# A hybrid block with latent attention: heads in pairs, scores two heads ahead, and q and k heads laid out over all 128 rows

## The chip, the cores and the metric

The kernel runs on one core of one Trainium2 chip. The metric is the device time of one execution in microseconds. The median of 3 runs of the kernel before is 1793.98 us (1790.98 to 1795.46). TensorE (PE) multiplies matrices into the eight banks of PSUM, VectorE (DVE), ScalarE (ACT) and GpSimd (POOL) work on tiles of 128 rows, and SyncE (SP) issues most of the loads.

## The reference, cut to what matters

Two layers follow each other: a first block (gated linear attention, a state space layer, a feed-forward network) and a second block. The change is in the second block's attention, with 512 tokens, 8 heads, 64 plain and 32 rotated dimensions for each head of q and k, and 64 for v. Beside it runs a depthwise convolution with a layer norm. In words, from the reference:

```python
q, kv = rmsnorm(q_lat, q_norm_g) @ w_uq, rmsnorm(kv_lat, kv_norm_g) @ w_ukv   # 384 -> 8*96, 256 -> 8*128
q_pe, k_pe = apply_rope(q[..., 64:96], cos, sin), apply_rope(k_rope, cos, sin)  # k_pe is one for all heads
s = jnp.einsum('bhqd,bhkd->bhqk', q_blk, k) * 96 ** -0.5
p = jax.nn.softmax(jnp.where(mask, s, neg), axis=-1)                            # mask: position of the key <= that of the query
o = jnp.einsum('bhqk,bhkd->bhqd', p, v)                                         # then @ w_o_attn
def apply_rope(x, cos, sin):
    x1, x2 = jnp.split(x, 2, axis=-1)
    return jnp.concatenate([x1 * cos - x2 * sin, x2 * cos + x1 * sin], axis=-1)
```

The attention output and the normed, gated (silu) convolution each go through a projection of 512 to 1024 (`oa` and `oc` below), are gated, added and go through `w_out` (`wo2`). A mixture of experts ends the block.

## The kernel before, in words

All weights come in units of 128x2048 through a ring of three tiles, in the order of `PLAN` (around the change: ga, gc, uq 0, uq 1, kv 0, oa 0, oa 1, oc 0, oc 1, wo2). Each unit is split into a high and a low part: ScalarE copies the high part (`high`, L953), then VectorE or POOL subtracts it (`low`, L1557). POOL does it for ga, gc, uq and kv, VectorE for oa, oc and wo2. A product then is three matmuls, high x high, high x low, low x high (`three`). The high and low parts have two places, used in turn, so the high part of a unit can be written once the unit two before it is used. `next_high(name, i)` and `next_low(name, i)` stand where the split of the unit after `name, i` is issued.

Every engine has its own program in a fixed order, written out by hand: `tensor`, `scalar`, `vector`, `gpsimd`, `sync`. Nothing is moved past a wait. Each instruction signals by name (`sig`) and others wait for the name (`at`). `Banks` gives out the PSUM banks, the one closed longest ago first; the taker waits until the last reader of the old tile has freed it. One bank, `conv`, is VectorE's accumulator for the convolution until `banks.close("conv")`.

The stretch around the change, in order:

- *q.* TensorE makes 8 tiles of 128x512, one for each head: rows 0 to 63 the plain dimensions, 64 to 95 the rotated, 96 to 127 the rotated with halves exchanged. ScalarE copies the first 64 rows to `QH` (L1383). VectorE multiplies rows 64 to 95 by the cosine and 96 to 127 by the signed sine and adds them (`rope`, L2167, L2168, L2170). POOL copies the rotated k to all heads (L2605) between its two weight splits.
- *k.* TensorE makes 8 tiles of 64x512, ScalarE copies them to `KH` (L1387).
- *Scores.* `scores(h)` makes 4 tiles of 128 queries x 512 keys in fp32; a fp32 matmul shows in the trace as two passes. `v2` follows scores(0).
- *Softmax.* On VectorE `soften(h)` scales and masks (L2225), takes the row maximum (L2228) and negates it (L2230), for each tile; ScalarE takes the exponential with the sum (L1393); VectorE normalises (L2235, L2238).
- *Output.* TensorE transposes the probabilities (L769, 16 for a head), ScalarE copies them to `PT` (L1405), TensorE multiplies by v into half of a bank (`pv`); two heads fill it, and ScalarE and VectorE take its high and low part (L1410, L2263).
- In the loop over heads TensorE does scores(h + 1), then the transposes of h, then the product with v of h.
- *Convolution.* Its mean, centring (L2257), squares (L1414), variance, square root (L979), reciprocal (L1569), norm (L2245, L2247), sigmoid (L1422) and POOL's product (L2610) are spread over the heads. `cvh` and `cvl` are its high and low part.
- After the loop come oa (2 units), oc (2 units) and wo2 (4 units). The first unit of oa is consumed for each of the four pieces of the attention output as it comes.

Of the kernel before, what the change touches and what calls it, by code (L numbers as in the profile page):

```python
# [7 lines left out]
F32 = mybir.dt.float32  # L8
# [4 lines left out]
ALU = mybir.AluOpType  # L13
# [134 lines left out]
def program(nc, W, wmoe, mcst, vecs, cst, xT, wal, wgu, bc, rw, posr, posc, xslot, yslot, prep, bbar, ushuf, yshuf, out):  # L148
    ctx = ExitStack()
    with ctx:  # L150
# [64 lines left out]
        def con(name):  # L215
# [68 lines left out]
        PB = [[tile(f"probs{z}{m}", o, 512) for m, o in enumerate(oo)]  # L284
              for z, oo in enumerate(((14336, 14848, 15360, 15872), (16384, 21112, 22648, 23160)))]
        PT = [tile(f"probs_t{k}", 29816 + 512 * k, 512) for k in range(4)]
# [69 lines left out]
        ogf = RO["og"].rearrange("p m g -> p (m g)")  # L356

# [3 lines left out]
        def tensor(g):  # L361
# [367 lines left out]
            for h in range(8):  # L729
                b = fresh("kh", h)  # L730
                for k in range(2):
                    t = three(b[0:64, :], wh[:, k, 64 * h:64 * h + 64], wl[:, k, 64 * h:64 * h + 64], kvh[:, k, :], kvl[:, k, :], k == 0, k == 1)
                t.then_inc(*p.sig(("kh", h)))
                banks.close("kh", h)
            p.end("end", "heads", "pe")

            def scores(h):
                p.wait_ge(*at("kh_ready"))
                p.wait_ge(*at("rope_ready"))
# [14 lines left out]
            banks.close("conv")  # L754
            b = fresh("conv_mean")
# [5 lines left out]
            for h in range(8):  # L761
                z = h % 2
                if h < 7:
                    scores(h + 1)
                for kb in range(4):
                    b = fresh("pt", h, kb)
                    for m in range(4):
                        p.wait_ge(*at("probs", h, m))
                        t = g.transpose(b[:, 128 * m:128 * m + 128], PB[z][m][:, 128 * kb:128 * kb + 128], ident)  # L769
                    t.then_inc(*p.sig(("pt", h, kb), ("turned", h)))  # L770
                    banks.close("pt", h, kb)
                b = fresh("pv", h // 2) if h % 2 == 0 else banks.at("pv", h // 2)
                o = b[64 * (h % 2):64 * (h % 2) + 64, :]
                p.wait_ge(*at("v2_ready"))
                p.wait_ge(*at("probs_t", h))
                for kb in range(4):
                    t = mm(o, V2[:, kb, 64 * h:64 * h + 64], PT[kb], kb == 0, kb == 3)
                t.then_inc(*p.sig(("pv", h // 2), ("attended", h)))
                if h % 2:
                    banks.close("pv", h // 2)  # L780
                if h == 1:
# [164 lines left out]
        def scalar(g):  # L946
# [432 lines left out]
            for i in range(2):  # L1379
                next_high("uq", i)  # L1380
                for h in range(4 * i, 4 * i + 4):
                    a.wait_ge(*at("uq", h, 0))
                    g.activation(QH[0:64, h, :], banks.at("uq", h, 0)[0:64, :], ACT.Copy).then_inc(*a.sig(("uq_out", h)))  # L1383
# [1487 lines left out]
```

## Time and profile before

| what | value |
|---|---|
| median of 3 runs | 1793.98 us |
| span of the profiled execution (its own time is not given apart from it) | 1789.8 us |
| TensorE busy | 1691.9 us, 95% |
| VectorE busy | 1219.3 us, 68% |
| ScalarE busy | 744.2 us, 42% |
| POOL busy | 352.4 us, 20% |
| mean granted TensorE clock | 0.973 |

The profile is one execution. The span goes from its first to its last instruction. A busy share is an average over stages with different limits, so the stages are read one by one, in windows of us from the start of the span.

### The profile page before, as it was taken

The page shows a single profiled execution, that of the slowest core. Times are in us where ns is not written, and L with a number is a line of the kernel's source. Part 1 is how long each engine was busy: PE and PEld are TensorE (multiplying, and loading weights), DVE is VectorE, ACT ScalarE, POOL GpSimd, SP SyncE. Part 2 cuts the span into 40 slices and gives each one's busy share as a digit, 9 for nine tenths or more (in the row PEclk, how much of TensorE's full clock was granted, in tenths as well). Part 3 has the DMA queues.
Part 4 walks back from the last instruction along what each step waited for, and adds up shares of the span by engine and source line. Part 5 has one row for each costly group of instructions (what it writes and reads, how often), then busy time and mean ns, then how long its engine had stood idle before and what let it go on. Part 6 is the DMA issues. An engine that isn't in the chain of part 4 may idle for free. (4 is left out here: it accounts for less than half of the span.)

```text
span 1789.8 us, 19686 instructions
## 1 busy us (share of the span) xinstructions
PE 1691.9 (95%) x8122; PEld 1330.9 (74%) x8122; DVE 1219.3 (68%) x1585; ACT 744.2 (42%) x962; POOL 352.4 (20%) x193
## 2 busy tenths in 40 slices
PE   6999899899999989999999989999898998999997
PEld 5778777677888868888878877878543776777775
DVE  5979768963333349843555446959786565999998
ACT  5253445444222342222222224342466235777774
POOL 1000012114000004200000014433200002555552
PEclk8999999999999999999999969999998999999999
DMA  6425222423322324434435402222100104999995
GB/s 231 182 100 181 75 73 72 160 82 129 118 94 94 128 84 164 165 133 184 153 143 186 165 24 78 94 93 94 71 0 1 71 24 157 397 380 385 384 367 192
DMA packets 59641, 264.51 MB, mean 148 GB/s; under 512 B 21648, under 2 KB 22288, under 8 KB 33056
## 3 DMA queue, kind: packets, MB, share of 16 engines
q1 hardware_dynamic: 34896, 159.10, 24.3%
q0 software_dynamic: 15184, 99.90, 14.2%
q10 hardware_dynamic: 9472, 4.26, 0.8%
q8 instruction: 64, 1.05, 0.2%
q14 instruction: 25, 0.20, 0.0%
HBM read 239.80 MB, written 23.44 MB: 147 GB/s over the span
## 5 line engine op out<-in xcount | busy, mean ns | idle before, releaser
L372 PE MATMUL bank<-h_high,wsplit 128*128 128x512 f32 x992 | 321.6, 402 | 10.9 <-ACT h_high L1283 4.9
L1557 DVE TENSOR_TENSOR wsplit<-ring,wsplit 128x2048 fp32r<-128x2048 f32 x75 | 174.3, 2324 | 160.4 <-ACT wsplit L953 160.4
L953 ACT ACTIVATE wsplit<-ring 128x2048 fp32r<-128x2048 f32 x98 | 187.0, 1908 | 210.8 <-PE bank L372 198.1
L372 PEld LDWEIGHTS bank<-h_high,wsplit 128*128 128x128 f32 x992 | 189.1, 191 | 57.4 <-ACT h_high L1283 5.0
L372 PE MATMUL bank<-xn_high,wsplit 128*128 128x512 f32 (+1 forms) x832 | 218.0, 349 | 11.3 <-DVE xn_low L1588 8.0
L372 PE MATMUL bank<-h_low,wsplit 128*128 128x512 f32 x496 | 198.1, 399 | 0.0
L372 PEld LDWEIGHTS bank<-xn_high,wsplit 128*128 128x128 f32 x832 | 146.2, 191 | 33.8 <-DVE xn_low L1588 8.1
L372 PE MATMUL bank<-f_high,wsplit 128*128 128x512 f32 x512 | 168.2, 401 | 0.0
L372 PE MATMUL bank<-xn_low,wsplit 128*128 128x512 f32 (+1 forms) x416 | 144.2, 347 | 0.0
L1557 POOL TENSOR_TENSOR wsplit<-ring,wsplit 128x2048 fp32r<-128x2048 f32 x23 | 106.3, 4622 | 179.1 <-ACT wsplit L953 178.9
L2620 POOL DMA_INDIRECT ring<-in_wmoe,indices x42 | 84.4, 2010 | 187.3 <-DVE routing L2362 135.3
L2579 POOL TENSOR_TENSOR x<-x,z 128x512 f32<-128x512 f32 x8 | 11.5, 1441 | 552.8 <-DVE z L2032 552.8
L372 PEld LDWEIGHTS bank<-f_high,wsplit 128*128 128x128 f32 x512 | 96.3, 188 | 21.9
L372 PEld LDWEIGHTS bank<-h_low,wsplit 128*128 128x128 f32 x496 | 94.9, 191 | 22.3 <-issue 0.2
L372 PE MATMUL bank<-f_low,wsplit 128*128 128x512 f32 x256 | 101.2, 395 | 0.0
L2157 DVE SCALAR_TENSOR_TENSOR bank<-conv_in,vecs,bank 128x512 f32<-128x512 f32 x116 | 87.7, 756 | 4.1
L372 PEld LDWEIGHTS bank<-xn_low,wsplit 128*128 128x128 f32 x416 | 79.4, 191 | 10.7 <-issue 1.0
L372 PE MATMUL bank<-m_high,wsplit 128*128 128x512 f32 x256 | 81.4, 396 | 3.8 <-DVE wsplit L1557 2.9
L372 PE MATMUL bank<-g_high,wsplit 128*128 128x512 f32 x256 | 80.8, 395 | 0.0
L372 PE MATMUL bank<-wsplit,block_high 128*128 128x512 f32 x232 | 76.2, 410 | 0.6 <-DVE block_low L2419 0.6
L1293 ACT ACTIVATE f_high<-norm_tmp 128x512 fp32r<-128x512 f32 x32 | 20.3, 634 | 123.5 <-DVE norm_tmp L2091 123.5
L372 PE MATMUL bank<-parts,block_high 128*128 128x512 f32 x216 | 68.9, 400 | 0.0
(496 smaller groups left out, 3398.9 us busy)
## 6 DMA issues: line engine op xcount, KB each, us to landing
ring<-in_W SPq DMA_DIRECT2D x122, 1024.0 KB, 4.8
weights_out<-prep SPq DMA_DIRECT2D x8, 864.0 KB, 5.4
prep<-weights_out_early POOLq DMA_DIRECT2D x8, 576.0 KB, 3.1
xslot<-zeros SPq DMA_DIRECT2D x7, 516.0 KB, 5.1
block<-xslot SPq DMA_DIRECT2D x6, 516.0 KB
yslot<-block_out SPq DMA_DIRECT2D x6, 512.0 KB, 9.1
prep<-turns_early POOLq DMA_DIRECT2D x8, 288.0 KB, 2.4
x_in<-in_xT SPq DMA_DIRECT2D x4, 528.0 KB, 7.4
```

Of the source, the lines that this page charges most:

```text
L372: return g.matmul(o, l, r, start=first, stop=last_, skip_group_check=True)
L953: g.activation(wst[:, side(n), 0, :], ringt[:, n % RING, :], ACT.Copy).then_inc(*a.sig(("high", n)))
L1293: g.activation(fh[:, j % 16, :], nrm[:, 2 * z, :], ACT.Square).then_inc(*a.sig(("f_high", j)))
L1557: g.tensor_tensor(wst[:, side(n), 1, :], ringt[:, n % RING, :], hi, SUB).then_inc(*t.sig(("low", n), ("released", n)))
L2157: g.scalar_tensor_tensor(out=o, in0=i, scalar=cw[:, c, k:k + 1], in1=grown, op0=MUL, op1=ADD).then_inc(*v.sig(("convolved",), ("free", "co ...
L2579: g.tensor_tensor(X[:, k, :], X[:, k, :], Z[:, k, :], ADD).then_inc(*q.sig((name, "x", k)))
L2620: g.indirect_dma_start(slots[c % NS], None, wmoe, indexed(x)).then_inc(slot_landed[c % NS], 16)
```

## The change

It does the following.

- q: the columns of `w_uq` are laid out by fours of heads: one tile with the rotated dimensions of four heads (4 x 32 rows), one with the exchanged ones, two with the plain ones of two heads each. VectorE multiplies the first two over 128 rows, and adds by head. ScalarE copies the plain ones, freeing the banks.
- k: 4 products with 128 columns in place of 8 with 64.
- Softmax: one `tensor_tensor_reduce` for each tile makes the negated, scaled and masked scores and their minimum; the exponential takes them with a scale of -1.
- The loop goes by pairs of heads. Scores run two heads ahead, probabilities have 10 tiles in place of 8, turned ones 8 in place of 4, and both heads' products with v alternate between the halves of a bank.
- The convolution's root is taken after head 5 (the variance is copied plainly before), its norm after the last normalise, and its sigmoids after the loop. The split of oa 1 moves into the loop.

```diff
-        PB = [[tile(f"probs{z}{m}", o, 512) for m, o in enumerate(oo)]
-              for z, oo in enumerate(((14336, ...), (16384, ...)))]
-        PT = [tile(f"probs_t{k}", 29816 + 512 * k, 512) for k in range(4)]
+        PB = [tile(f"probs{k}", o, 512) for k, o in enumerate((14336, 14848, ... 28280))]       # 10
+        PT = [tile(f"probs_t{k}", o, 512) for k, o in enumerate((29816, 30328, ... 29304))]     # 8
+        def probs(h, m):
+            return PB[(4 * h + m) % 10]
 tensor:
-            for h in range(8):
-                b = fresh("kh", h)
+            for j in range(4):
+                b = fresh("kh", j)
                 for k in range(2):
-                    t = three(b[0:64, :], wh[:, k, 64 * h:64 * h + 64], ...)
+                    t = three(b, wh[:, k, 128 * j:128 * j + 128], ...)
 ...
             banks.close("conv")
+            scores(1)
             b = fresh("conv_mean")
 ...
+            def attend(pr):
+                b = fresh("pv", pr)
+                p.wait_ge(*at("v2_ready"))
+                p.wait_ge(*at("probs_t", 2 * pr + 1))
+                for kb in range(4):
+                    for e in range(2):
+                        h = 2 * pr + e
+                        t = mm(b[64 * e:64 * e + 64, :], V2[:, kb, 64 * h:64 * h + 64], PT[4 * e + kb], kb == 0, kb == 3)
+                        if kb == 3:
+                            t.then_inc(*p.sig(("pv", pr), ("attended", pr)))
+                banks.close("pv", pr)
+            for pr in range(4):
+                for h in (2 * pr, 2 * pr + 1):
+                    turn_probs(h)                      # the 16 transposes
+                    if h < 6:
+                        scores(h + 2)
+                attend(pr)
+                if pr == 1:                            # conv_var
 scalar:
+                    j, e = 4 * i + 2 + (h % 4) // 2, h % 2
+                    g.activation(QH[0:64, h, :], banks.at("uq", j, 0)[64 * e:64 * e + 64, :], ACT.Copy)
 ...
             soften(0)                                  # V2 copies follow
+            soften(1)
             for h in range(8):
+                probs_out(h)                           # the 4 copies to PT
+                if h < 6:
+                    soften(h + 2)
                 if h % 2:
+                    a.wait_ge(*at("attended", h // 2)) # copy to ath
+                if h == 1:                             # 4 squares of the convolution, then
+                    next_high("oa", 0)
+                elif h == 3:
+                    g.activation(rs, banks.at("conv_var"), ACT.Copy)
+                elif h == 5:
+                    g.activation(rs, rs, ACT.Sqrt, scale=1.0 / 512, bias=eps)
+            for c in range(4):                         # the 4 sigmoids
+                g.activation(nrm[:, c % 3, :], CO[:, c, :], ACT.Sigmoid)
             a.wait_ge(*at("end", "attention", "pe"))   # 4 copies to cvh
-            for i in range(2):
-                next_high("oa", i)
+            next_high("oa", 1)
 vector:
-                for h in range(4 * i, 4 * i + 4):
-                    rope(QH[64:96, h, :], banks.at("uq", h, 0), ("free", "uq", h, 0))
+                for z in range(2):
+                    g.tensor_tensor(KP[:, z, :], banks.at("uq", 4 * i + z, 0), TR[:, z, :], MUL)
+                for e in range(4):
+                    r = slice(32 * e, 32 * e + 32)
+                    g.tensor_tensor(QH[64:96, 4 * i + e, :], KP[r, 0, :], KP[r, 1, :], ADD)
 ...
-                    g.scalar_tensor_tensor(out=pb, in0=banks.at("s", h, m), scalar=96.0 ** -0.5, in1=MK[:, m, :], op0=MUL, op1=ADD)
-                    g.tensor_reduce(mx, pb, AX, MAX)
-                    g.tensor_scalar(mx, mx, -1.0, None, MUL)
+                    if n > 9:                          # n = 4 * h + m
+                        v.wait_ge(*at("turned", (n - 10) // 4))
+                    g.tensor_tensor_reduce(out=probs(h, m), in0=banks.at("s", h, m), in1=MK[:, m, :], scale=-(96.0 ** -0.5), scalar=-BIG,
+                                           op0=ADD, op1=ALU.min, accum_out=st[:, z, m:m + 1])
 ...
             soften(0)
+            soften(1)
+            for pr in range(4):
+                normalise(2 * pr)
+                normalise(2 * pr + 1)
+                if pr == 0:                            # wait for conv_mean, centre 4 tiles
+                else:                                  # low part of pair pr - 1
+                if pr == 1:
+                    next_low("oa", 0)
+                if pr < 3:
+                    soften(2 * pr + 2)
+                    soften(2 * pr + 3)
+            for c in range(4):
+                conv_norm(c)
+            v.wait_ge(*at("at_high", 3))               # low part of pair 3
+            oa_out(0)                                  # then the 4 low parts of the convolution,
+            next_low("oa", 1)                          # then
+            oa_out(1)
```

## Rows read from the trace of the kernel before

**Rows 1.** The page: busy time of the engines.

```profile
PE 1691.9 (95%) x8122; PEld 1330.9 (74%) x8122; DVE 1219.3 (68%) x1585; ACT 744.2 (42%) x962; POOL 352.4 (20%) x193
```

**Rows 2.** Windows of stages: busy us (instructions) by engine, granted clock, DMA.

```profile
1250.00:1268.00 18.00, 15.97 (x68) 12.17 (x66) 14.84 (x12) 7.87 (x10) 13.33 (x3) 1.00 0.16 59
1268.00:1283.00 15.00, 12.24 (x49) 6.18 (x49) 13.20 (x17) 6.91 (x11) 0.02 (x1) 1.00 0.19 71
...
1298.00:1386.00 88.00, 76.62 (x252) 35.45 (x251) 65.98 (x132) 57.38 (x111) 5.43 (x4) 0.94 0.00 0
...
1386.00:1409.00 23.00, 23.00 (x99) 18.54 (x100) 12.89 (x15) 6.47 (x8) 0.00 (x0) 1.00 0.26 92
```

**Rows 3.** Timeline of PE, k products and first scores: start us, us.

```profile
1268.36 0.39 PE L372 MATMUL bank<-kv_low,wsplit 128*64 128x512 f32 x1
...
1274.70 0.44 PE L372 MATMUL bank<-kv_high,wsplit 128*64 128x512 f32 x1 [0.67 <-DVE rope_tmp L2168]
...
1282.90 3.70 PE L372 MATMUL bank<-kh,qh 96*128 96x512 f32 x8 [0.68 <-ACT kh L1387]
```

**Rows 4.** Timeline of POOL in the head of the stretch.

```profile
1254.44 4.57 POOL L1557 TENSOR_TENSOR wsplit<-ring,wsplit 128x2048 fp32r<-128x2048 f32 x1 [9.53 <-ACT wsplit L953]
1259.16 3.86 POOL L2605 COPY kh<-k_pe 32x4096 f32<-32x4096 f32 x1 [0.15 <-POOL wsplit L1557]
1263.10 4.92 POOL L1557 TENSOR_TENSOR wsplit<-ring,wsplit 128x2048 fp32r<-128x2048 f32 x1
```

**Rows 5.** Timeline of DVE there: end of the convolution, rope, the split.

```profile
1251.57 0.75 DVE L2157 SCALAR_TENSOR_TENSOR conv<-conv_in,vecs,bank 128x512 f32<-128x512 f32 x1
...
1256.40 3.16 DVE L2170 TENSOR_TENSOR qh<-rope_tmp 32x512 f32<-32x512 f32 x1
...
1279.93 2.29 DVE L1557 TENSOR_TENSOR wsplit<-ring,wsplit 128x2048 fp32r<-128x2048 f32 x1
```

**Rows 6.** Timeline of PE in the loop: one head, and the last two.

```profile
1305.22 3.70 PE L372 MATMUL bank<-kh,qh 96*128 96x512 f32 x8
1308.75 1.91 PE L769 MATMUL bank<-cst,probs 128*128 128x128 f32 x16
1311.51 3.65 PE L372 MATMUL bank<-probs_t,v 128*64 128x512 f32 x8 [0.85 <-ACT probs_t L1405]
1315.09 3.70 PE L372 MATMUL bank<-norm_tmp,cst 128*128 128x512 f32 x8
...
1375.88 3.64 PE L769 MATMUL bank<-cst,probs 128*128 128x128 f32 x16 [1.36 <-DVE probs L2238]
1380.21 5.70 PE L372 MATMUL bank<-probs_t,v 128*64 128x512 f32 x8 [0.69 <-ACT probs_t L1405]
```

**Rows 7.** Windows at the end of the loop, as rows 2.

```profile
1378.00:1380.00 2.00, 1.52 (x8) 1.12 (x6) 0.00 (x0) 1.49 (x3) 0.00 (x0) 0.50 0.00 0
```

**Rows 8.** Groups by line from 1282 to 1386: busy, mean ns, idle before.

```profile
L2228 DVE TENSOR_REDUCE small<-probs 128x1 f32<-128x512 f32 x32 | 22.0, 686 | 1.1
L2225 DVE SCALAR_TENSOR_TENSOR probs<-bank,mask 128x512 f32<-128x512 f32 x32 | 21.8, 682 | 3.3 <-PE bank L372 3.3
...
L2238 DVE TENSOR_SCALAR probs<-probs,small 128x512 f32<-128x512 f32 x32 | 16.4, 576 | 0.3
...
L1393 ACT ACT_TABLE_LOAD x6 | 7.7, 1283 | 0.1
L1393 ACT ACTIVATION_READ_ACCUMULATOR probs<-probs,small 128x1 f32 x32 | 6.1, 192 | 0.0
...
L1422 ACT ACT_TABLE_LOAD x4 | 5.1, 1283 | 0.1
...
L1569 DVE RECIPROCAL norm_tmp<-norm_tmp 128x512 f32<-128x512 f32 x1 | 3.3, 3343 | 0.0
```

**Rows 9.** Timeline of ACT in the head of the stretch: copies of q.

```profile
1254.18 1.65 ACT L1383 ACTIVATE qh<-bank 64x512 f32<-64x512 f32 x3
```

**Rows 10.** The state products of the first block (`into`): timeline of PE.

```profile
277.49 1.15 PE L372 MATMUL bank<-u_shuffled,g_turned 128*64 128x65 f32 x32
```

More of the change, by code:

```diff
@@ L738, in scores @@
                 p.wait_ge(*at("kh_ready"))
+                p.wait_ge(*at("nope_ready"))
                 p.wait_ge(*at("rope_ready"))
@@ L760, in tensor, with turn_probs @@
             banks.close("conv_mean")
[L761 to L764, printed above, removed]
+            def turn_probs(h):
                 for kb in range(4):
@@ L2210, in vector @@
                 next_low("uq", i)
-                for h in range(4 * i, 4 * i + 4):
-                    v.wait_ge(*at("uq", h, 0))
-                    v.wait_ge(*at("uq_out", h))
-                    rope(QH[64:96, h, :], banks.at("uq", h, 0), ("free", "uq", h, 0))
+                for z in range(2):
+                    v.wait_ge(*at("uq", 4 * i + z, 0))
+                    v.wait_ge(*v.own())
+                    g.tensor_tensor(KP[:, z, :], banks.at("uq", 4 * i + z, 0), TR[:, z, :], MUL).then_inc(*v.sig(("free", "uq", 4 * i + z, 0)))
+                v.wait_ge(*v.own())
+                for e in range(4):
+                    r = slice(32 * e, 32 * e + 32)
+                    g.tensor_tensor(QH[64:96, 4 * i + e, :], KP[r, 0, :], KP[r, 1, :], ADD).then_inc(*v.sig(("rope_ready",)))
             next_low("kv", 0)
@@ L2251, in vector @@
             soften(0)
-            for h in range(8):
-                normalise(h)
-                if h == 0:
+            soften(1)
[3 more added lines that the diff above has]
+                if pr == 0:
                     v.wait_ge(*at("conv_mean"))
@@ L2276, in vector @@
                     g.tensor_tensor(GA[:, j, :], banks.at("oa", j, 0), GA[:, j, :], MUL).then_inc(*v.sig(("free", "oa", j, 0)))
+            oa_out(0)
+            for c in range(4):
+                v.wait_ge(*at("cv_high", c))
+                g.tensor_tensor(cvl[:, c, :], CO[:, c, :], cvh[:, c, :].bitcast(F32), SUB).then_inc(*v.sig(("cv_split", c)))
+            next_low("oa", 1)
+            oa_out(1)
             for i in range(2):
@@ L2826, in layout @@
     q = a["w_uq_2"][0].reshape(384, 8, 96)
-    q = lay(np.concatenate([q, q[:, :, 80:96], q[:, :, 64:80]], axis=2).reshape(384, 1024), 512)
+    turned_q = np.concatenate([q[:, :, 80:96], q[:, :, 64:80]], axis=2)
+    q = lay(np.concatenate([x[:, 4 * i:4 * i + 4].reshape(384, -1) for i in range(2) for x in (q[:, :, 64:96], turned_q, q[:, :, 0:64])], axis=1), 512)
     parts["uq"] = np.concatenate([q, np.zeros((2, 128, 512), np.float32)], axis=2)
```

98 lines of the change are left out of this document (39 added, 59 removed).

## The prediction, before the changed kernel was run

> **What bounds the kernel now.** I read the page first: TensorE is busy for 95% of the span, so time is won only where it waits or does less [rows 1]. Then the windows, one for each stage around the change. The reader is to see that TensorE is full until 1250, has gaps from 1250 to 1283 (15.97 of 18 us, 12.24 of 15 us) and in the attention loop (76.62 of 88 us, at a granted clock of 0.94), and is full again from 1386 to 1409 [rows 2]. So about 137 us, from the first q product at 1248.5 to the first product of the attention output at 1385.8, are where this change can act; what runs after it is a chain of its own.
>
> Then the timelines of the engines in that stretch. **Head of the stretch:** the k products start at 1268.08, when POOL has split their weights, and three of them wait 0.67 us for VectorE's rope to free a bank [rows 3, 4]. The scores start at 1282.90 behind the last k copy [rows 3]. VectorE does three rope instructions for each head, on 32 rows. Three of the sums take 2.4 to 3.4 us where 512 elements take 0.68 (L2225) [rows 8], and each ends 0.54 us after a POOL instruction ends (1259.56 after 1259.01, 1263.57 after 1263.02, 1268.56 after 1268.02) [rows 4, 5]: a sum of two SBUF tiles stands still while POOL works. **Loop:** a head costs TensorE 3.5 us of scores, 1.8 us of transposes, 0.9 us of waiting for the copies of the turned probabilities and 3.55 us of products with v (1305.22, 1308.75, 1311.51, 1315.09) [rows 6]: 9.9 us. 8 of these, with 5.5 us for v2 and twice 3.5 us for the convolution's mean and variance, would be 91.5 us; the stretch from 1282.9 to 1385.8 is 102.9. The other 11 us are waits for normalised probabilities, and a half clock at the end: the same 16 transposes take 3.64 us and the same products 5.70 us, with the granted clock at 0.50 (the 1.2 GHz level) after a wait of 1.4 us and several of about 1 us [rows 6, 7]. The waits come from VectorE: 0.68 + 0.69 + 0.15 us, 1.51 us from start to start, for each of 32 score tiles, and from ScalarE's ten table loads of 1.28 us [rows 8].
>
> **The change part by part.** I make a schedule from durations of rows.
>
> *Rope and k.* VectorE: 24 instructions become 4 products of 0.69 us and 8 sums of 0.68 us. It is done with the convolution at 1252.3, and its first two products end at 1253.8 [rows 5]. Of the first four sums, at worst one gets through between two POOL instructions, so they end at 1259.6, 1263.6 and 1268.6; the next two products and four sums take 6 x 0.72 us, to 1272.9, and the split of oa's first unit, 2.29 us, ends at 1275.2. TensorE: the k products start at 1268.07 as before, since POOL's chain of 4.57, 3.86 and 4.92 us sets that and is not touched. There are 24 instead of 48, at 0.233 us (1268.36 to 1269.05 is three of them): they end at 1273.7, and the banks that they take are free by 1269.3. ScalarE: the last q tile is there just before the k products start, two copies follow, the split of the next unit runs from 1268.8 to 1270.7, then 8 copies at 0.55 us (three took 1.65) [rows 9], to 1275.1. So the scores start at 1275.1, set by ScalarE's copies; VectorE is free when the first score tile is ready, over 1 us after (two passes). Gain 7.8 us.
>
> *Softmax.* Three instructions for a tile become one that reads the same PSUM tile and mask and also writes the row minimum. The trace shows no such instruction. Below: it can't be quicker than the 0.68 us of L2225, which is the same read and write. Above: a second pass, 0.68 + 0.69. Nearest is L2225, with a small read of the sum as ScalarE has (0.19 us, L1393) [rows 8]. I take 0.8 us. The Trainium skill ("VectorE: DVE Perf Modes", Two Vector instructions with no wait between them) says that an instruction that also gives out its accumulator is two, the second a read without input. No row of VectorE shows it; by it the whole would be 1 to 2 us longer, within the range.
>
> *Products with v.* They go in pairs of heads, alternately into rows 0 to 63 and 64 to 127 of a bank: 16 passes for a pair. The trace before has one place with such alternation, the state products of the first block (`into`): 32 passes of 65 columns in 1.15 us, so (1.15 - 0.22) / 31 = 0.030 us each, 0.46 ns a column. The products with v, not alternating, run at 0.43 us for 512 columns, 0.84 ns a column [rows 6, 10]. So two halves of the array run side by side, at 1.8 times the rate. Two ends: 16 x 512 x 0.46 = 3.8 us for a pair, or 16 x 0.43 = 6.9 us. I take the 3.8, as the alternation there is the same, though its passes are short. The Trainium skill ("TensorE: Matmul & The Clock Gate", Part 3: Packing small matmuls) gives 2.38 times for three column tiles. By that efficiency two tiles would give 1.6 times and 4.4 us for a pair, 2 us more in the whole.
>
> *Order.* Scores run two heads ahead, so the copies of the turned probabilities lie behind scores, except for the last pair. ScalarE's table loads between exponentials go: the root's value is copied plainly and the four sigmoids come after the loop. The final normalisation of the convolution (reciprocal 3.34 us, then four times two instructions, 1.25 us) moves behind the last normalise.
>
> *The sum*, from the start of the scores, T = 0. TensorE: scores 0 to 3.5, v2 to 9.0, scores to 12.4, mean to 15.8. VectorE has softened head 1 by 13.7 and normalised head 0 by 15.5 (four of L2238, 0.58 us in the mean with POOL's products in the way, and a small reciprocal; I take 1.9 us a head, without POOL [rows 8]), so nothing waits. Turn, scores, turn, scores, pair 0: 17.6, 21.1, 22.8, 26.3, 30.1. Head 2's probabilities are ready at 29.8: turn to 31.9, scores to 35.3. Here ScalarE is late: it has copied pair 0's output (31.2), squared four tiles (33.4) and split oa's second unit (35.3) before it copies head 2's turned tiles (37.4), exponentiates head 4 (41.3) and copies head 3's (43.4). Pair 1 can't start before 43.4, where TensorE would have been ready at about 41.5: to 47.2. Variance 50.7; turn, scores, turn, scores, pair 2: 52.4, 55.9, 57.6, 61.1, 64.9. VectorE finishes head 7's scores at 62.5 and its normalise at 66.3: turns to 66.6 and 68.4. ScalarE has the root with its table load until 67.6, then eight copies, as those of q some 0.5 us each: 71.8. Pair 3 ends at 75.7. I add 1.3 us for semaphore steps that I left out: 77. The half clock at the end I expect once more, because TensorE waits 3.5 us there; at half speed over the last pair and its neighbours it costs 2 us, where before it cost (3.64 - 1.91) + (5.70 - 3.62) and 1.4 us more on head 6, 5.2 us inside the 102.9. That gives 79.
>
> *After the loop* nothing is won. The convolution's chain now starts at the end of the loop: table load 1.28, sigmoid 0.63, four POOL products of 1.4 and the copies are done 9 us later, VectorE's lows after oa's first outputs at 17, and the split of oc's first unit at 19.3, while oa's 96 products keep TensorE until 22.5 as now. Cover is 3 us; if it were gone, each us would cost one.
>
> So 7.8 + 102.9 - 79 = 31.7 us; I say 31. The profiled execution had a span of 1789.8 us, 4.2 under the median of 1793.98 us of the runs shown; only its span is given. The stretch is the same in both, so I take the gain from the median: 1763 us.
>
> **The rivals.** *The halves of the array do not overlap* in long fp32 passes that accumulate: 4 x (6.9 - 3.8) = 12.4 us more, all on TensorE's path, as ScalarE's late chain starts from pair 0's end and moves with it. 1775 us. For it: the only row with overlap has passes of 65 columns. Against it: the rate there. Chance 0.18.
> *VectorE's new instruction takes two passes* (1.4 us): a pair costs it 8 x 1.4 + 3.8 + 0.7 = 15.7 us against TensorE's 14.3 us, so VectorE sets the loop; stretch near 83, 1768 us. Chance 0.10.
> *The convolution's chain becomes the end*: 6 us more after the loop, if ScalarE's sigmoids or POOL's products wait longer than summed: 1769 us. Chance 0.06.
> *Slower*: the new instruction runs at the pace of the reciprocal, 3.34 us for 128x512 [rows 8]. With 32 on VectorE's path the loop is 81 us at 1.5 us each and 32 us longer for each us more: the gain is gone from 2.4 us on, and at 3.34 the stretch is 140 us, 1823 us. Nothing else that reads PSUM takes so long here. Chance 0.04.
> The forecast itself: 0.62.
>
> **How the numbers follow.** A measurement of this kernel can't tell less than 0.3%, 5.4 us, from no change; that bound is 1788.6 us. The forecast's own range is 1757 to 1768 (instruction 0.68 to 1.0 us, half clock none or twice). To take in both middle rivals and the first one with 3 us to spare the range is 1755 to 1778. Faster 0.93: the forecast, the three milder rivals but for 0.03 where several of these costs add up to no change; slower 0.04.
>
> **What would show each step right or wrong.** The k products as 24 and scores starting near 1275 (not 1283). Rope sums stretched by POOL only up to 1268.6. A pair's products, 16 passes, in about 4 us, not 7. The new VectorE instruction under 0.9 us. Three table loads in the stretch, not ten or more. TensorE's first oa product near 1354, with its one longer wait ahead of the last pair; oc's first product 22.5 us after it, without a wait. Wrong would be a VectorE busy throughout the loop, or a TensorE wait on the convolution's lows.

## The result, and the profile after

The changed kernel takes 1758.14 us (median of 4 runs) where the kernel before took 1792.74 us beside it (4 runs): a ratio of 0.9822, with a 95% interval of 0.9803 to 0.984. The prediction was 1763 us, in a range of 1755 to 1778. The profiled execution took 1757.74 us, with a span of 1755.7 us.

The page of the changed kernel, busy time of the engines, to be set beside [rows 1]:

```profile
span 1755.7 us, 19580 instructions
...
PE 1664.1 (95%) x8098; PEld 1322.3 (75%) x8098; DVE 1189.1 (68%) x1541; ACT 735.0 (42%) x955; POOL 340.0 (19%) x193
```

TensorE has the same share of a shorter span, so what it does got shorter too, by 27.8 us. The timeline of TensorE after the change, in the stretch from the first q product to the first product of oa (start us, us, instruction, number; in brackets the wait and who ended it), answers to [rows 3, 6]:

```profile
1268.58 0.50 PE L376 MATMUL bank<-kv_high,wsplit 128*128 128x512 f32 x1 [0.36 <-POOL wsplit L1583]
...
1276.27 3.70 PE L376 MATMUL bank<-kh,qh 96*128 96x512 f32 x8 [1.83 <-ACT kh L1404]
...
1302.65 3.65 PE L376 MATMUL bank<-probs_t,v 128*64 128x512 f32 x16
1306.23 1.97 PE L773 MATMUL bank<-cst,probs 128*128 128x128 f32 x16
...
1313.84 3.70 PE L376 MATMUL bank<-kh,qh 96*128 96x512 f32 x8 [0.33 <-DVE small L2255]
1318.82 3.65 PE L376 MATMUL bank<-probs_t,v 128*64 128x512 f32 x16 [1.28 <-ACT probs_t L1419]
...
1339.98 3.71 PE L773 MATMUL bank<-cst,probs 128*128 128x128 f32 x32
1346.80 5.16 PE L376 MATMUL bank<-probs_t,v 128*64 128x512 f32 x16 [3.10 <-ACT probs_t L1419]
1351.88 22.66 PE L376 MATMUL bank<-attn,wsplit 128*128 128x512 f32 x96
```

Three things are to be seen. Sixteen passes of probabilities by v, for two heads, take 3.58 us from start to start (1302.65 to 1306.23), as long as eight took before. The reader can tick off the long waits: one of 1.83 us ahead of the scores, one of 1.28 us ahead of pair 1, and one of 3.10 us ahead of pair 3, all for ScalarE's copies. Pair 3 then runs at half clock, 5.16 instead of 3.65 us. Its windows show it (us from the start; busy us of each engine with the number of instructions, granted clock, DMA):

```profile
1346.00:1352.00 6.00, 5.20 (x17) 1.69 (x18) 4.82 (x9) 0.66 (x2) 0.00 (x0) 0.72 0.00 0
1352.00:1375.00 23.00, 23.00 (x99) 18.54 (x100) 10.30 (x14) 8.90 (x12) 5.19 (x4) 1.00 0.14 46
```

VectorE's timeline after, for the rope's sums, the split of oa's first unit, and the new instruction (L2255):

```profile
1254.39 14.68 DVE L2244 TENSOR_TENSOR qh<-rope_tmp 32x512 f32<-32x512 f32 x4
...
1270.70 2.83 DVE L2244 TENSOR_TENSOR qh<-rope_tmp 32x512 f32<-32x512 f32 x4
1273.57 2.29 DVE L1583 TENSOR_TENSOR wsplit<-ring,wsplit 128x2048 fp32r<-128x2048 f32 x1
...
1313.70 0.68 DVE L2255 CUSTOM_DVE_ANT_0 probs<-bank,mask 128x512 f32<-128x512 f32 x1
1314.31 0.08 DVE L2255 DVE_READ_ACCUMULATOR2_ANT small<- 128x1 f32 x1
```

The first four sums take 14.68 us beside POOL's three instructions, the next four, with POOL idle, 2.83 us. The fused instruction is 0.68 us of work and 0.08 us to read the minimum. The next tile's work starts 0.61 us after it where nothing holds VectorE.

How the stretches compare is the key to all that follows, so they are set out once. All are differences of start times on TensorE's timeline of one profiled execution each. Times of the whole are less sharp: the first q product comes between 1246.26 and 1253.45 us in the 12 profiles, though no kernel here changes anything ahead of it that was meant to take time.

| kernel | time, us | first q product | to first scores | from there to first oa product | from there to the end of the span |
|---|---|---|---|---|---|
| before | 1792.74 | 1248.73 | 34.17 | 102.93 | 404.0 |
| after | 1758.14 | 1249.15 | 27.12 | 75.61 | 403.8 |
| e1, not alternating | 1767.99 | 1252.06 | 27.11 | 84.00 | 403.5 |
| e2, three instructions | 1771.94 | 1253.45 | 27.12 | 85.38 | 404.7 |
| e3, old heads | 1765.82 | 1253.31 | 34.17 | 75.81 | 403.9 |
| e4, heads only | 1784.71 | 1250.42 | 27.11 | 99.77 | 403.9 |
| e5, fused only | 1787.75 | 1250.10 | 34.19 | 97.83 | 403.0 |
| e6, order alone | 1775.52 | 1248.27 | 28.67 | 95.55 | 402.5 |
| e7, late root | 1755.19 | 1247.67 | 27.12 | 72.16 | 404.4 |
| e8, all moves | 1752.28 | 1249.16 | 27.06 | 70.18 | 403.4 |
| e9, scores per head | 1747.43 | 1246.26 | 26.06 | 69.98 | 402.8 |
| e10, passes per copy | 1749.60 | 1252.89 | 25.13 | 68.77 | 403.6 |

One run of e1 (2073.95 us, mean granted clock 0.744) and one of e5 (2302.36 us, 0.675) were slow: they are in the medians of the table, which would be 1767.26 and 1787.52 us without them, and not in the ratios below.

The result in these terms: 7.05 us come from the head of the stretch and 27.32 us from the loop, 34.4 us, and nothing from what follows. The spans differ by 34.1 us, the medians by 34.6 us.

### The profile page after: what moved, and what is told of

Read it like the earlier page. It is cut to its first block and busy times, and to the rows that moved or that the text cites. A ratio compares the mean times of both kernels' runs of the same rounds, so it can differ in the third digit from the quotient of the medians.

```text
span 1755.7 us, 19580 instructions
## 1 busy us (share of the span) xinstructions
PE 1664.1 (95%) x8098; PEld 1322.3 (75%) x8098; DVE 1189.1 (68%) x1541; ACT 735.0 (42%) x955; POOL 340.0 (19%) x193
## 3 DMA queue, kind: packets, MB, share of 16 engines
q1 hardware_dynamic: 34896, 159.10, 25.1%
## 5 line engine op out<-in xcount | busy, mean ns | idle before, releaser
L376 PE MATMUL bank<-h_high,wsplit 128*128 128x512 f32 x992 | 320.6, 401 | 10.8 <-DVE h_low L2070 4.9
L2617 POOL TENSOR_TENSOR x<-x,z 128x512 f32<-128x512 f32 x8 | 11.6, 1444 | 554.3 <-DVE z L2058 554.3
L376 PEld LDWEIGHTS bank<-xn_low,wsplit 128*128 128x128 f32 x416 | 79.0, 190 | 10.8 <-issue 1.0
```

The lines of the kernel that those rows point to most:

```text
L376: return g.matmul(o, l, r, start=first, stop=last_, skip_group_check=True)
L2617: g.tensor_tensor(X[:, k, :], X[:, k, :], Z[:, k, :], ADD).then_inc(*q.sig((name, "x", k)))
```

## The experiments

The first four kernels ran on one chip beside the kernel before (1790.41 us, 13 runs), e5 to e8 on another (1789.24 us, 15 runs), e9 and e10 in a third set (1788.35 us, 9 runs). Ratios are to the kernel before on the same chip, with the 95% interval.

### e1: a pair's heads one after the other

```diff
-                for kb in range(4):
-                    for e in range(2):
+                for e in range(2):
+                    for kb in range(4):
```

> The changed kernel, with the 4 products of the even head done before the 4 of the odd one, as before the change. If TensorE's own work sets the loop and the alternation runs two halves of the array at once, a pair's 16 passes take 7.1 us from start to start instead of 3.6, four times, so 14 us more: 1772 us, the stretch from the first scores to the first oa product 89.6 us instead of 75.6. If the softmax chain sets the loop, TensorE's waits before pair 1 (1.3 us) and pair 3 (3.1 us) and more would swallow part: 10 us more or less. If the passes were quick for another reason than the alternation, 3.6 us stays.

1767.99 us, ratio 0.9868 (0.9847 to 0.9889). The loop is 8.4 us longer than after, and not the 14 of my first case. A pair takes 5.35 us from start to start (1305.55 to 1310.90). TensorE's weight loads of that pair (start us, us, number in the group) say why:

```profile
1306.89 0.14 PEld L376 LDWEIGHTS bank<-probs_t,v 128*64 128x64 f32 x1 [0.29 <-issue]
1307.32 0.19 PEld L376 LDWEIGHTS bank<-probs_t,v 128*64 128x64 f32 x3 [0.29 <-issue]
1307.75 0.19 PEld L376 LDWEIGHTS bank<-probs_t,v 128*64 128x64 f32 x2 [0.23 <-issue]
1308.18 0.19 PEld L376 LDWEIGHTS bank<-probs_t,v 128*64 128x64 f32 x2 [0.23 <-issue]
1308.66 0.14 PEld L376 LDWEIGHTS bank<-probs_t,v 128*64 128x64 f32 x1 [0.29 <-issue]
```

Every 0.43 us one load, but from 1307.32 on there are two or three, and then one again. The rows do not name the head, but one load in each of these steps makes up the first head's eight, and the other four must be the second head's, for the other half of the array. The passes themselves start likewise: two at 1307.32, then at 1307.75 and 1307.80, 1308.18 and 1308.23, 1308.60 and 1308.66, and from 1309.09 on one each 0.43 us. So four of the sixteen passes run beside others without any alternation: 12 steps of 0.43 us, 5.2 us, where with alternation there are 8 steps. Of the 8.4 us, 1.8 are in each of the first three pairs, and the rest in the last one, which runs at half clock in both kernels (8.35 against 5.16 us). That the halves overlap is shown, and the overlap does not even need the alternation to begin. Why it begins four passes ahead, and not earlier, stays open.

### e2: three softmax instructions in the new order

The exponential's scale of -1 goes back with them.

```diff
-                    g.tensor_tensor_reduce(out=probs(h, m), in0=banks.at("s", h, m), in1=MK[:, m, :], scale=-(96.0 ** -0.5), scalar=-BIG,
-                                           op0=ADD, op1=ALU.min, accum_out=st[:, z, m:m + 1])
+                    g.scalar_tensor_tensor(out=pb, in0=banks.at("s", h, m), scalar=96.0 ** -0.5, in1=MK[:, m, :], op0=MUL, op1=ADD)
+                    g.tensor_reduce(mx, pb, AX, MAX)
+                    g.tensor_scalar(mx, mx, -1.0, None, MUL)
```

> The changed kernel, with scaling and mask, row maximum and negation as three VectorE instructions again. A tile costs VectorE 1.51 us instead of 0.61 to 0.86, a pair 8 x 1.51 + 3.6 + 0.7 = 16.4 us against TensorE's 14.0 us. If TensorE's work set the loop, VectorE now does: 8 to 10 us more, 1767 us. If the gain of the loop came mostly from the quicker softmax, it goes back by more than 15 us. If VectorE had slack all along, under 3 us.

1771.94 us, ratio 0.9909 (0.9878 to 0.9941). The loop is 9.8 us longer than after, in the 8 to 10 expected. The whole is 5 us above the 1767 expected; in the profile 4.3 us of that lie ahead of the first q product. VectorE now sets the loop's pace, as TensorE's timeline shows: scores wait for it tile by tile, and pair 1 waits for what follows from it.

```profile
1324.56 1.12 PE L376 MATMUL bank<-kh,qh 96*128 96x512 f32 x2 [0.18 <-DVE probs L2256]
1326.07 1.12 PE L376 MATMUL bank<-kh,qh 96*128 96x512 f32 x2 [0.38 <-DVE probs L2256]
...
1331.36 5.15 PE L376 MATMUL bank<-probs_t,v 128*64 128x512 f32 x16 [2.67 <-ACT probs_t L1419]
```

From 1324.56 to 1326.07 is 1.51 us, VectorE's pace for a tile with three instructions [rows 8].

### e3 and e4: the heads' layout alone

e3 is the changed kernel with the old layout of q and k, e4 is the kernel before with the new one:

```diff
-            for h in range(8):
-                b = fresh("kh", h)
+            for j in range(4):
+                b = fresh("kh", j)
```

and with it the tables of q's columns, VectorE's rope and ScalarE's copies, as in the change (e4; e3 the other way).

> The changed kernel, with q and k laid out and handled as before (8 q tiles with rope for each head, 8 k tiles of 64 rows). The scores start at 1283 instead of 1276, and the loop is the same: 7 us more, 1765 us. Rival: the head of the stretch is hidden, as the loop has its own end set by the convolution or by ScalarE: under 2 us.

> The kernel before with the new layout of q and k alone. If the two halves of the change add up, 7 us less than before: 1786 us, scores at 1276, and the loop of 102.9 us the same from there. Rival: the start comes earlier, but the loop grows by what VectorE has to catch up (the split of oa's first unit now falls into the start of the softmax): 3 us less.

e3: 1765.82 us, ratio 0.986 (0.9841 to 0.9879). e4: 1784.71 us, ratio 0.997 (0.9955 to 0.9984). By the table the layout is worth 7.05 us of head in either kernel, and in the new order nothing more. In the old order the loop is 3.2 us shorter as well, where I had expected no change, but no part of that can be put down to the layout: it is where the waits and the half clock fell in the two profiles. TensorE's timeline of e4 at the end, to be set beside [rows 6]:

```profile
1365.16 5.57 PE L372 MATMUL bank<-probs_t,v 128*64 128x512 f32 x8 [0.78 <-ACT probs_t L1409]
1370.66 2.21 PE L770 MATMUL bank<-cst,probs 128*128 128x128 f32 x16
1373.72 3.65 PE L372 MATMUL bank<-probs_t,v 128*64 128x512 f32 x8 [0.84 <-ACT probs_t L1409]
```

The slow passes (5.57 us) stand one head earlier than in the kernel before, and cost 3.2 us in all (0.96 in the transposes ahead of them, 1.92 and 0.30) where before they cost 5.1. Behind them the wait of 1.36 us for normalised probabilities is gone, as the probabilities were normalised while the slow passes ran. Together that is the 3.2 us of the loop.

### e5: the fused instruction alone, in the old order

The kernel before with the instruction of e2's diff the other way round, and a scale of -1 in the exponential.

> The kernel before with one edit: VectorE's three softmax instructions become the one, as in the changed kernel. Order of the loop, layout of the heads and all else are old. Theory (TensorE bounds the loop): the waits for normalised probabilities go, and with them the half clock; heads one after the other without overlap of halves leave 8 x (3.7 scores + 6.9 probabilities by v) + 8 x 3.7 turning, some 94 to 96 us from first scores to first product of oa where before had 102.9. So about 8 us less than before: near 1784. Rival (ScalarE's reloading of tables and its chain through each head bound the old loop anyway): at most 3 us, near 1789.

1787.75 us (10 runs), ratio 0.999 (0.9977 to 1.0002): no change that can be told. My theory expected 8 us, the rival at most 3, and the rival has it. TensorE's timeline of two heads late in the loop:

```profile
1365.22 0.72 PE L769 MATMUL bank<-cst,probs 128*128 128x128 f32 x2
1367.02 2.04 PE L769 MATMUL bank<-cst,probs 128*128 128x128 f32 x14 [1.07 <-DVE probs L2235]
1369.99 3.62 PE L372 MATMUL bank<-probs_t,v 128*64 128x512 f32 x8 [0.94 <-ACT probs_t L1405]
1374.96 2.73 PE L769 MATMUL bank<-cst,probs 128*128 128x128 f32 x16 [1.36 <-DVE probs L2235]
1378.54 3.65 PE L372 MATMUL bank<-probs_t,v 128*64 128x512 f32 x8 [0.84 <-ACT probs_t L1405]
```

The waits for normalised probabilities are still there, 1.07 us (and once more at 1345.17) and, as before [rows 6], 1.36 us, with VectorE busy for 31.80 of 60 us (1292 to 1352) where before it had 49.23. Only a wait of 0.47 us, at 1332.85 in the kernel before, is gone. What VectorE, POOL and ScalarE did ahead of these waits (timelines of the same kernel):

```profile
1362.69 0.69 DVE L2260 TENSOR_TENSOR attn<-bank,attn 128x512 fp32r<-128x512 f32 x1 [6.09 <-ACT attn L1410]
1363.29 0.68 DVE L2242 TENSOR_TENSOR conv<-conv,norm_tmp 128x512 f32<-128x512 f32 x1
...
1364.68 2.68 DVE L2235 TENSOR_SCALAR probs<-probs,small 128x512 f32<-128x512 f32 x4
1365.30 1.38 POOL L2607 TENSOR_TENSOR conv<-conv,norm_tmp 128x512 f32<-128x512 f32 x1 [9.77 <-ACT norm_tmp L1422]
1365.48 1.48 DVE L2235 TENSOR_SCALAR probs<-probs,small 128x512 f32<-128x512 f32 x1
...
1369.86 1.28 ACT L1393 ACT_TABLE_LOAD   x1
...
1374.12 0.18 DVE L2232 RECIPROCAL small<-small 128x4 f32<-128x4 f32 x1 [4.32 <-ACT probs L1393]
```

VectorE stood idle for 6.09 us, until ScalarE had copied the pair's output, and only then came its queue: the low part of the pair, two instructions of the convolution, the reciprocal and the normalisation. So these waits do not come from how much VectorE does. They have two origins.

- *1.07 us, twice.* Of the four normalisations the third (the row at 1365.48, one of the four of the row at 1364.68) takes 1.48 us where the others take 0.48, while POOL multiplies for the convolution (1365.30 to 1366.68). TensorE has turned two blocks and waits for the third tile. The same third normalisation is stretched at 1343.63 in this kernel, and twice in the kernel before, each time beside POOL's product. VectorE's queue brings the two together: head 6's exponentials were done at 1362.17, before the low part and the convolution began.
- *1.36 us, once.* VectorE had waited 4.32 us for the exponentials, and ScalarE had loaded a table (1.28 us) between its copies and them.

No run took POOL's product or the table load alone out of the old order, so both origins are read from the timelines and not tested.

The profiled loop is 5.1 us shorter; 4.3 of them are the half clock, which cost the kernel before 5.1 us at its last two heads (3.35 for 2.04, 3.64 for 1.91, 5.70 for 3.65 us) and e5 0.8 (2.73 for 1.91). The medians are 1.7 us apart (1789.24 and 1787.52), so not all of this is there in every execution.

### e6: the order without the two others

The changed kernel with both edits of e1 and e2.

> The changed kernel with the three softmax instructions and with a pair's sixteen passes head by head: of the loop only the order (pairs, scores two heads ahead) is new; the layout of q and k stays new. Runs so far gave +9.8 us for the three instructions alone and +8.4 for the lost alternation alone, over 75.6 from first scores to first product of oa. Theory (the loop goes by whichever engine is slower in each pair): VectorE is slower with three instructions, so TensorE's longer passes hide behind it: 86 to 89 us, near 1773. Rival (both lie on one chain, as a pair's passes hold the scores that VectorE waits for): the costs add, 94 us, near 1780.

1775.52 us, ratio 0.9921 (0.9898 to 0.9943). The loop takes 95.55 us: the costs add (9.8 and 8.4 on top of 75.6 are 93.8), as the rival had it for the loop; the time of the whole lies between the two, nearer to my theory's 1773. My expectation that the longer passes would hide behind VectorE is wrong. One reason can be read, at one place: while TensorE runs pair 1's passes and the variance it makes no scores, and VectorE, the slower one, waits for the next ones.

```profile
1344.35 0.69 DVE L2256 SCALAR_TENSOR_TENSOR probs<-bank,mask 128x512 f32<-128x512 f32 x1 [4.92 <-PE bank L376]
```

Behind pair 0 VectorE waited for ScalarE's split instead (2.65 us, to 1319.75). Another reason is again the clock. Pair 1 takes 7.06 us (the granted clock is 0.50 from 1332 to 1334), and so does the last pair. The first scores take 5.40 us for 3.70. The head of the stretch, 28.67 us, has a half clock too, in q products from 1259.95 to 1263.59.

With e4 to e6 the four parts of the loop can be set out, all from about 100 us (e4's 99.8, with the new heads): the new order alone gives 4.2 us; with the fused instruction 15.8 (e1), with alternation 14.4 (e2), with both 24.2. In the old order the fused instruction gives at most 5.1, most of it clock.

The half clock is part of these figures. By the rows that are longer than the same rows elsewhere in the profiles, it takes about 6.1 us of e6's loop, 4.4 of e2's, 3.2 of e4's, 2.9 of e1's and 1.5 of the changed kernel's. Without it the order alone gives 7.1 us, and 15.5, 15.6 and 22.5 with the fused instruction, the alternation and both; the two costs still add, and a little more than that: 6.9 us for the three instructions, 7.0 for the lost alternation, 15.4 for both. "The order" itself is several things that no run takes apart: pairs, scores two heads ahead, and the table loads, VectorE's norm and POOL's products moved out of the loop.

### e7: the root behind the last copies

```diff
                 if h < 6:
                     soften(h + 2)
+                if h == 7:
+                    g.activation(rs, rs, ACT.Sqrt, scale=1.0 / 512, bias=eps)
-                elif h == 5:
-                    g.activation(rs, rs, ACT.Sqrt, scale=1.0 / 512, bias=eps)
...
-            for c in range(4):
-                conv_norm(c)
+            conv_norm(0)
...                                                    # low part of pair 3
+            for c in range(1, 4):
+                conv_norm(c)
```

> The changed kernel with the root of the variance of the convolution's norm moved behind ScalarE's last copies of turned probabilities, and VectorE's norm of rows 1 to 3 moved behind the low part of the last pair. In the changed kernel TensorE waits 3.10 us for the copies ahead of the last pair's passes and then runs them at half clock, 5.16 instead of 3.65 us. Theory (the root and its table load of 1.28 us hold these copies): the wait falls to about 1.3 us and the half clock goes too: 72.5 to 74 us from first scores to first product of oa where the changed kernel has 75.6, so near 1756. If the clock stays at half, 74.3. Rival: the norm now ends so late that oc's first product waits: the stretch is shorter, but oc's first product comes no earlier, and the time stays at 1758.

1755.19 us, ratio 0.9814 (0.9793 to 0.9835). The loop takes 72.16 us, 3.45 less than after and just under the 72.5 to 74 expected. The gain is read from this stretch: as times of the whole, the intervals of the two ratios (0.9803 to 0.984 for the changed kernel) overlap. TensorE's timeline of its end:

```profile
1338.50 3.71 PE L773 MATMUL bank<-cst,probs 128*128 128x128 f32 x32
1343.37 3.65 PE L376 MATMUL bank<-probs_t,v 128*64 128x512 f32 x16 [1.15 <-ACT probs_t L1419]
1346.95 22.67 PE L376 MATMUL bank<-attn,wsplit 128*128 128x512 f32 x96
1369.46 0.40 PE L376 MATMUL bank<-cv_high,wsplit 128*128 128x512 f32 x1
```

The wait of 3.10 us is now 1.15, and the pair runs at full clock: 1.95 and 1.5 us. The convolution's last norm ends at 1356.9 instead of 1351.0, and that is 9.9 us behind oa's first product where it was 0.9 us ahead of it. Yet oc's first product follows oa's after 22.51 us, as after (1351.88 to 1374.39). VectorE's timeline of the changed kernel shows what takes the delay up:

```profile
1361.36 2.72 DVE L2307 TENSOR_TENSOR gate_attn<-bank,gate_attn 128x512 f32<-128x512 f32 x4 [8.02 <-PE bank L376]
```

After its last low part VectorE waits 8.02 us for oa's first outputs, and only behind them come the convolution's low parts and the split of oc's first unit. In e7 the norms fill that wait. The split ends 16.8 us behind oa's first product in the changed kernel and 17.0 us in e7, so the cover ahead of oc, 22.5 us less these, is 5.7 and 5.6 us: it was real, and hardly spent.

### e8: the splits moved out of the way

```diff
-            next_high("kv", 0)                         # first unit of oa, ahead of the k copies
-            for h in range(8):
+            for h in (0, 2, 1, 3, 4, 6, 5, 7):         # the k copies
...
             soften(0)
+            next_high("kv", 0)
...
-                if h == 1: ... next_high("oa", 0)      # the second unit
+                if h == 3: ... next_high("oa", 0)
```

VectorE's halves of the two splits move with them, and the second four of q are copied in the order 0, 2, 1, 3. Based on e7.

> The kernel with the late root, and three moves more: the splits of the first piece of oa out of the stretch ahead of the scores to behind the first head's softmax; those of its second piece from pair 1 to pair 2; and ScalarE's copies of q and k in an order in which two copies that read the same half of the partitions follow each other. Theory: the scores start 0.8 us earlier or more (of ScalarE's chain 1.93 us of splitting goes, but the product's last copy must still come), the waits ahead of pair 1 lose about 1.6 us, the late root's gain stays: from first q product to first product of oa 4 to 5.5 us less than in the changed kernel, near 1753.5. Rival: VectorE waits for ScalarE's split before the second head's softmax, and the moved splits only show up as a wait elsewhere: no more than the late root alone gives.

1752.28 us (5 runs), ratio 0.9788 (0.9773 to 0.9804), whose interval overlaps e7's. The loop is 1.98 us shorter than e7's: both waits around pair 1 are gone. But the head of the stretch gained 0.06 us, not 0.8. ScalarE's timeline shows the reason:

```profile
1268.26 1.69 ACT L1399 ACTIVATE qh<-bank 64x512 f32<-64x512 f32 x3 [1.51 <-PE bank L376]
...
1271.67 2.31 ACT L1403 ACTIVATE kh<-bank 64x512 f32<-64x512 f32 x4 [0.81 <-PE bank L376]
1274.47 1.69 ACT L1403 ACTIVATE kh<-bank 64x512 f32<-64x512 f32 x3 [0.49 <-PE bank L376]
```

ScalarE now waits for TensorE's k products, and its last three copies can't start before the last product is there. Freed of the split, ScalarE is no longer late, but the scores wait for all eight copies.

### e9 and e10: waits for the part that is needed

```diff
             def scores(h):
-                p.wait_ge(*at("kh_ready"))
+                p.wait_ge(*at("kh_ready", h))
```

and, on top of it, in e10:

```diff
-                p.wait_ge(*at("probs_t", 2 * pr + 1))
                 for kb in range(4):
+                    p.wait_ge(*at("probs_t", 2 * pr + 1, kb))
```

> The kernel with all moves, and one edit: the scores of a head wait for the copies of k of that head, not of all eight. With all moves the scores still began 1.78 us after the last k product ended, because its three last copies (1.69 us) could only start then. Theory (this wait alone holds the scores): they start within 0.3 us of the k products, 1.6 to 2 us earlier, and 27.06 us from first q product to first scores become about 25.2; the time 1750.5. Rival: the next wait takes its place at once (the first table load, the softmax of head 0, the v product's banks), so that the scores start earlier but the first turning does not: 1752.3 as with all moves.

> The kernel with scores per head, and one more edit: a pair's passes of v wait for each block of turned probabilities as its copy is made, not for all four of the second head. In the kernel with all moves TensorE waited 1.15 us for the last copy ahead of the last pair's passes. Theory: the first passes start as the last pair's turning ends, since three of the second head's four copies are done or in hand by then, and 0.6 to 1.1 us of the wait goes; 1749.7. Rival: the later passes wait in their place for the last copies (each copy takes 0.5 us, each pair of passes 0.45 us), so less than 0.3 us is won.

e9: 1747.43 us (5 runs), ratio 0.9772 (0.9746 to 0.9798). e10: 1749.60 us (5 runs), ratio 0.9779 (0.9755 to 0.9803). TensorE's timeline of e10:

```profile
1277.79 0.39 PE L376 MATMUL bank<-kv_high,wsplit 128*128 128x512 f32 x1
1278.02 3.60 PE L376 MATMUL bank<-kh,qh 96*128 96x512 f32 x8
...
1339.57 3.71 PE L773 MATMUL bank<-cst,probs 128*128 128x128 f32 x32
1343.21 3.65 PE L376 MATMUL bank<-probs_t,v 128*64 128x512 f32 x16
1346.79 22.67 PE L376 MATMUL bank<-attn,wsplit 128*128 128x512 f32 x96
```

From the last k product to oa TensorE waits for nothing any more; e10's 93.9 us from first q to first oa product are 8.8 less than after. The theory of each run holds in its stretch: e9's scores start right behind the last k product, and e10's last pair behind the turning, 1.2 us earlier in the loop, a little more than the 0.6 to 1.1 expected. In e9 the head is 26.06 us, not 25.1, as some q products ran at half clock (one of 0.73 us at 1256.66, where it takes 0.50 in e8 and e10). That e10 is not the faster of the two as a whole is not explained by its stretch, which is 2.1 us shorter: its first q product comes 6.6 us later than e9's, after stages that are alike in both. The page's windows differ there in the clock. From 50 to 100 us e10 has a granted clock of 0.93 and e9 0.97. What makes the clock of the early stages differ from profile to profile stays open. So e9 and e10 together are the best version, 8 to 11 us below the changed kernel by the medians and by the ratios (the interval of e9 lies below that of the changed kernel, that of e10 touches it), and which of them is better can't be told.

## Why the prediction was right

The time came out 4.9 us under the forecast of 1763. The gain was 34.6 us where 31 was said, and the other 1.2 us are the kernel before, 1792.74 us beside the changed one where the forecast starts from 1793.98. By its own steps, each with what the runs showed:

- **Head of the stretch**, predicted 7.8 us, measured 7.05. The rope's sums were held by POOL to 1269.07 (1268.6 in the sum), the k products are 24 and start at 1268.58, and ScalarE's copies set the scores, as said. The term that was off is these copies: eight at 0.55 us were taken, from three that read the same half of the rows; they alternate between the halves of a bank and take 0.62 us each (4.92 for eight), 0.5 us more in all. e3 and e4 give the same 7.05 us in both orders.
- **The new instruction**, taken at 0.8 us, is 0.69 with its read, and the next one starts 0.61 us after it. The rival with two passes (1.4 us) falls. The Trainium skill's rule ("VectorE: DVE Perf Modes", Two Vector instructions with no wait between them) is borne out in form: there is a second record, the read of the accumulator, but it takes 0.08 us.
- **Products with v**, taken at 3.8 us for a pair, are 3.58: the overlap is exactly twofold, the one row of 65 columns was the right witness, and the rival without overlap falls. Its price of 12.4 us was not tested: e1 lost 8.4 us, but four of each pair's passes still ran beside others there.
- **The loop**, predicted 79 us, measured 75.6. This is the term that makes up most of the miss. Up to the end of pair 0 the schedule is right to 0.2 us (T = 29.96, said 30.1). ScalarE's late chain let pair 1 start at 42.6, not 43.4, and pair 3 started at 70.5, not 71.8. The 1.3 us that I added for semaphore steps were not there: every step of the schedule was taken from start to start, so they were in it already. The half clock cost 1.5 us, said 2.
- **The last wait**, 3.5 us said, 3.10 measured, has ScalarE's root with its table load (1.28 us at 1340.74) in it, as said; e7 takes 1.95 us of it away and leaves 1.15 us for the copies. Three table loads are left, at 1276.24, 1340.74 and, just behind the stretch, 1352.63.
- **After the loop** nothing was won, as said. The split of oc's first unit, said to end 19.3 us behind oa's first product, ends 16.8 us behind it, so the cover is 5.7 us and not 3. It holds in e7, where the last norm ends 10.8 us later against oa.
- **The sum**: 7.05 + 27.32 = 34.4 against 7.8 + 23.9 = 31.7, 0.7 less and 3.4 more; and 0.7 was rounded off.

One reading of the profile before was wrong in part, and the forecast did not suffer. The waits for normalised probabilities in the old loop were put down to VectorE's 1.51 us a tile and ScalarE's table loads. e5 shows that all but 0.47 us of them stay when VectorE does 0.6 us a tile. The table loads can stand for the wait of 1.36 us, and the two of 1.07 us fall beside POOL's product, which the prediction saw only as a longer mean of the normalisations. The forecast did not suffer because the parts were priced on the new schedule, where loads and products lie outside the loop. No sum of single parts on the old one would have given 27 us: there the fused instruction is worth 1.7 us by the medians, and the order alone 4 us of the loop.

## What to carry to other kernels

Lay out the new schedule engine by engine, from start to start, before pricing an edit: the same fused instruction was worth nothing that could be told in an order in which its engine waited, and 11.6 us of the loop (e6 against e1, about 3 of them half clock) in one in which its engine set the pace without it. When a schedule has become tight, look for waits that ask for more than the next instruction needs: an engine's wait for all copies where one is enough cost 1 to 2 us at two places here, and a root ahead of eight copies 3.4, of which 1.5 were half clock. Compare stretches inside a profile, not only whole times, when effects are near 0.3%: the stages ahead moved by up to 7.2 us between profiles of kernels that are alike there.

## What the hardware showed that was not expected

- Matmul passes into the two halves of the array start beside each other also when they are not issued in turn: in e1 the second head's first pass started at 1307.32, beside the first head's fifth, and with it four of the sixteen ran beside others.
- Scaling, mask and minimum over 128x512 out of a PSUM bank in one instruction go at 0.61 us from start to start, with 0.08 us for the accumulator's read, where ScalarE's read takes 0.19.
- ScalarE's copies of 64x512 tiles start 0.62 us apart when they alternate between the halves of the rows that they read (4.92 for eight), and 0.50 us apart when two that read the same half follow each other. The three copies of 1.69 us in e8 have one of each.
- A normalisation of 128x512 in SBUF on VectorE took 1.48 us beside a product on POOL (1.38 us), and 0.48 us without it (e5); that stood for two waits of TensorE of 1.07 us.
- The half clock appeared after different waits in kernels with the same work: after a wait of 3.10 us in the changed kernel, not after one of 1.15 in e7, and in one head or the next in e4 and before. In e2 the wait of 2.67 us ahead of pair 1 is followed by slow passes (5.15 us), and the one of 2.60 us ahead of pair 0 by passes of 3.65 us and slow transposes behind them (2.83 us for 1.91). Where it appeared in the loop it was worth 0.8 (e5) to 6.1 us (e6).
